# Latent attention's deferred layer-norm scale and shift: four 128x1024 passes written for GpSimd instead of VectorE

## What is computed

```python
def layer_norm(x, g, b):
    xf = x.astype(F32)
    mu = jnp.mean(xf, -1, keepdims=True)
    var = jnp.mean(jnp.square(xf - mu), -1, keepdims=True)
    return ((xf - mu) * lax.rsqrt(var + LN_EPS) * g + b).astype(x.dtype)

def modulated_sublayer(x, mod, g, b, fn, res_w):
    shift, scale, gate = mod[:, 0, None, :], mod[:, 1, None, :], mod[:, 2, None, :]
    y = fn(x * (1.0 + scale) + shift)
    return layer_norm(DEEPNORM_ALPHA * x + res_w * (1.0 + gate) * y, g, b)

def mla(h, pos, w_down, q_norm, kv_norm, w_uq, w_ukv, w_out):
    cq, ckv, kr = jnp.split(h @ w_down, [C_Q_RANK, C_Q_RANK + C_KV_RANK], axis=-1)
    q = (rms_norm(cq, q_norm) @ w_uq).reshape(bsz, seq, C_HEADS, C_NOPE + C_ROPE)
    kv = (rms_norm(ckv, kv_norm) @ w_ukv).reshape(bsz, seq, C_HEADS, C_NOPE + C_V)
    ...   # rope on part of q and on kr, softmax attention over 16 heads, two blocks of 128 queries
    return o.swapaxes(0, 1).reshape(bsz, seq, C_HEADS * C_V) @ w_out
```

## Time and profile before

| what | value |
|---|---|
| time, median of 3 runs | 1033.8 us (1032.54 to 1034.34) |
| span of the profiled execution | 1031.5 us |
| PE busy in the span | 999.8 us (97%) |
| DVE busy | 805.0 us (78%) |
| ACT busy | 501.1 us (49%) |
| POOL busy | 47.5 us (5%) |
| latent attention, from its first transposes to the next sublayer's | about 721 to 841 us of the span |

### The profile page before, as it was taken

The page is one execution under the profiler, slowest core; times in us unless marked ns, Lnnn a source line. Parts: engine busy times, 40 slices in busy tenths (PEclk is TensorE's granted clock), DMA queues, the critical chain, the costliest instruction groups (busy, mean ns, idle before and its releaser), DMA issues.

```text
span 1031.5 us, 13182 instructions
## 1 busy us (share of the span) xinstructions
PE 999.8 (97%) x5024; PEld 830.8 (81%) x5024; DVE 805.0 (78%) x1192; ACT 501.1 (49%) x749; POOL 47.5 (5%) x101
## 2 busy tenths in 40 slices
PE   7999999999999999999999999999999999999996
PEld 5678888879978788888887888888878878888885
DVE  5989898678989888888879788877787786666455
ACT  3654344376767534343445343443666654443430
POOL 1000000002311000000000000000000010000000
PEclk9999999999999999999999999999999999999998
DMA  9999998458423699979758987972323449756431
GB/s 353 409 352 410 386 374 321 152 184 287 164 95 125 210 370 350 329 272 341 272 176 332 328 304 277 387 261 93 97 93 123 166 166 312 239 199 245 163 123 41
DMA packets 72545, 254.80 MB, mean 247 GB/s; under 512 B 8801, under 2 KB 10337, under 8 KB 72482
## 3 DMA queue, kind: packets, MB, share of 16 engines
q1 hardware_dynamic: 68946, 242.91, 65.4%
q0 software_dynamic: 3104, 10.39, 3.1%
q10 hardware_dynamic: 432, 0.66, 0.2%
HBM read 252.85 MB, written 1.07 MB: 246 GB/s over the span
## 4 chain that ended last, share of the span: by engine, by line
PE 81%; DVE 7%; ACT 4%; issue 3%; DMA 3%; SPq 0%; POOL 0%; DVEq 0%; ACTq 0%; POOLq 0%
PE bank L1769 25%; PE bank L1773 25%; PE bank L1772 25%; DMA w_raw<-in_w_dram 2%; PE bank L2170 2%; DMA arena<-in_ada_w_dram 1%; DVE w_lo L1156 1%; ACT w_hi L851 1%; PE bank L1995 1%; ACT arena L866 1%; PE bank L1913 1%; PE bank L1880 1%; PE bank L1764 1%; PE bank L2025 0%; DVE arena L1173 0%
## 5 line engine op out<-in xcount | busy, mean ns | idle before, releaser
L1156 DVE TENSOR_TENSOR w_lo<-w_raw,w_hi 128x2048 fp32r<-128x2048 f32 (+3 forms) x161 | 345.0, 2162 | 27.6 <-ACT w_hi L851 27.6
L1769 PE MATMUL bank<-w_hi,hT_hi 128*128 128x512 f32 (+3 forms) x880 | 350.0, 398 | 12.7 <-DVE hT_lo L1201 6.2
L1773 PE MATMUL bank<-w_lo,hT_hi 128*128 128x512 f32 (+3 forms) x880 | 338.8, 385 | 0.0
L1772 PE MATMUL bank<-w_hi,hT_lo 128*128 128x512 f32 (+3 forms) x880 | 338.4, 385 | 0.0
L851 ACT ACTIVATE w_hi<-w_raw 128x2048 fp32r<-128x2048 f32 (+3 forms) x152 | 281.1, 1852 | 36.0 <-DMA w_raw<-in_w_dram 25.8
L1769 PEld LDWEIGHTS bank<-w_hi,hT_hi 128*128 128x128 f32 x880 | 166.0, 189 | 48.4 <-DVE hT_lo L1201 7.4
L1773 PEld LDWEIGHTS bank<-w_lo,hT_hi 128*128 128x128 f32 x880 | 165.8, 188 | 33.2
L1772 PEld LDWEIGHTS bank<-w_hi,hT_lo 128*128 128x128 f32 x880 | 166.4, 189 | 28.8
L936 ACT ACTIVATE arena<-bank 128x256 f32<-128x256 f32 x88 | 33.7, 383 | 290.2 <-PE bank L1773 290.1
L1173 DVE SCALAR_TENSOR_TENSOR arena<-arena,c_row 128x1024 f32<-128x1024 f32 x131 | 155.9, 1219 | 8.4 <-DMA arena<-in_ada_w_dram 8.3
L1769 PE MATMUL bank<-w_hi,fT_hi 128*128 128x512 f32 x352 | 138.1, 392 | 0.9 <-DVE fT_lo L1679 0.9
(11 more groups left out here) (235 smaller groups left out, 858.0 us busy)
## 6 DMA issues: line engine op xcount, KB each, us to landing
w_raw<-in_w_dram SPq DMA_DIRECT2D x306, 512.0 KB, 5.5
arena<-in_ada_w_dram SPq DMA_DIRECT2D x132, 512.0 KB, 7.3
m_o<-in_ada_w_dram SPq DMA_DIRECT2D x10, 512.0 KB, 7.1
gate_row<-gate_scratch POOLq DMA_DIRECT2D x6, 512.0 KB, 4.8
arena<-in_ln_g_dram POOLq DMA_DIRECT2D x6, 512.0 KB, 4.9
arena<-in_ln_b_dram POOLq DMA_DIRECT2D x6, 512.0 KB, 6.9
w_raw<-in_w_dram SPq DMA_DIRECT2D x8, 256.0 KB, 2.8
w_raw<-in_w_dram SPq DMA_DIRECT2D x8, 192.0 KB, 2.8
```

What stands on the lines that cost most here:

```text
L1156: op = nc.vector.tensor_tensor(w_lo[:, j0 % RING, c], raw_of(j0)[:, c], w_hi[:, j0 % RING, c].bitcast(F32), ALU.subtract)
L1769: mm = nc.tensor.matmul(dst, a_hi, b_hi, start=start, stop=False)
L1772: nc.tensor.matmul(dst, a_lo, b_hi, start=False, stop=False)
L1773: return nc.tensor.matmul(dst, a_hi, b_lo, start=False, stop=stop)
```

## The change

The stage `scale` is taken out of VectorE's list and put into GpSimd's. The four operations, their shapes and their operands are the same.

```diff
                             nc.gpsimd.tensor_tensor(rms[:, 2 * t:2 * t + 2], ssq[:, 2 * t:2 * t + 2],
                                                     neg_half[:, 0:1].broadcast_to([P, 2]), ALU.pow).then_inc(rms_ready, 1)
+                        elif stage == "scale":
+                            t, part = m
+                            pool.wait_ge(n_tr, 4 * s + 2 * t + 2)
+                            pool.wait_ge(ln_rows_in, 32 * s)
+                            step.wait()
+                            op = nc.gpsimd.tensor_tensor(x[:, t, :], x[:, t, :], ln_rows[:, part, :], (ALU.mult, ALU.add)[part])
+                            if part == 0:
+                                step(op)
+                            else:
+                                op.then_inc(x_ready, 1)
                 ln_tail(s)
...
                     elif stage in ("split", "lo"):
                         split_lo(base[s] + m[0], m[1:])
-                    elif stage == "scale":
-                        t, part = m
-                        if part == 0:
-                            dve.wait_ge(ln_rows_in, 32 * s)
-                            step(nc.vector.tensor_tensor(x[:, t, :], x[:, t, :], ln_rows[:, 0, :], ALU.mult))
-                            scaled = step.n
-                        else:
-                            dve.wait_ge(dve_step, scaled)
-                            nc.vector.tensor_tensor(x[:, t, :], x[:, t, :], ln_rows[:, 1, :], ALU.add).then_inc(x_ready, 1)
                     elif stage == "end":
```

## The result

The changed kernel takes **1039.96 us** (median of 5 runs, 1037.95 to 1040.89) against 1033.93 (5 runs beside it): 1.0056 times as long, 95% interval 1.0046 to 1.0067. It is slower by 6.0 us, where 2.8 were forecast; the time lies 1.2 us above the end of the range.

A forecast was written before the change was run, and what follows sets the result against it. TensorE, busy for 97% of the span, was taken as the bound. A slip of +4.0 us from two held rotations less a gain of 1.2 gave +2.8, so 1036.6 us, range 1032.4 to 1038.8.

The forecast's parts named there:

- the gain: Before the transposes at 762.82 us, TensorE's 1.17 us gap closes once VectorE's passes go: 1.2 us gained, bounds 0 and 2.2.
- The cause and its places: GpSimd's reads hold VectorE's two-SBUF-input operations; TensorE idles about 2 us before the product at 743.93 and the transposes at 748.65.
- The first pass: From 742.71 us it holds VectorE's L1608 in the first rotation by 2.0 us; TensorE's product at 743.93 slips by 2.0.
- The passes' length: Each 128x1024 two-input pass on GpSimd takes 2.2 us, between 1.2 and 2.44.
- The second rotation: It begins at 748.3 us; the third pass holds its L1608 by 2.0; the transposes at 748.65 slip 4.0 in all.
- The held remainder: Weight remainder L1156, 745.29 us before, waits for the second pass until 747.4 and ends at 748.3; costed at nothing by itself.
- the rival of three holds: Third pass admitted before the second rotation, fourth before its L1608: 6.0 - 1.2 = +4.8 us, 1038.6; chance 0.13.
- The scans of the earlier trace: VectorE's L1422 took 0.68 to 0.90 us beside GpSimd's L787 at 0.55 to 1.42; read as GpSimd losing more.
- The rival of hardly any loss: VectorE's operations win nearly each time and its slack takes in the rest; only the gain stays: -1.2 us, 1032.6; chance 0.20.
- one hold only: First pass enters after L1608; only the second rotation's L1608 is held, by 2.0 us: +0.8 us, 1034.6; chance 0.22.

The follow-up runs named there:

- e2: The changed kernel with GpSimd's four passes left out and four fills of 128x2048 that only write SBUF in their place: 1032.53 us.
- e3: The kernel before, VectorE keeping its passes, with four operations of the same shape added on GpSimd, whose results nobody needs: 1041.49 us.
- e5: The changed kernel with each GpSimd pass made to wait for the maximum of a later attention step (9, 10, 11 and 14): 1032.41 us.
- e7: The changed kernel with each GpSimd pass cut into two operations of 512 columns, eight in all: 1036.79 us.
- e4: The changed kernel with 12 and 20 extra TensorE products in front of the two places where it waits for VectorE: 1038.79 us.
- e11: The changed kernel as it is, run once more without extra products: 1039.12 us.
- the half change: The change for the first tile alone: GpSimd does the first two passes, VectorE keeps the last two where they were: 1035.58 us.

## Why the prediction was wrong

*What bounds the kernel, and the gain: right.* The gap of 1.17 us closed and nothing else did; 1.2 was forecast, the kernel without passes gives 1.4 and the marks 1.34.

*The cause and its places: right.* VectorE's rotations are held in the two stretches named, and TensorE waits at the two instructions named. The holds come from GpSimd's reads (e2 and e3).

*The first pass: right in size.* Forecast 2.0, measured 2.17 on TensorE. GpSimd got in one operation earlier, between the two L1606 (the second starts at 743.97 and takes 2.39 us) and not in the pause before L1609: here VectorE operations that follow closely were no protection.

*The passes' length: mis-sized a little.* 2.2 us was taken; a pass beside which VectorE read PSUM or stood idle took 2.35 to 2.40 (e5), near the upper end of 2.44. The fixed part of the operation is small: two of 512 columns take 2.52 us (e7).

*The second rotation: the step that failed.* The forecast let one pass, the third, hold this rotation, by 2.0 us, and put the fourth, which was to meet the next weight remainder, at nothing. Instead the third pass got in ahead of the rotation's first operation (L1604, +1.63) and the fourth between its next two (L1606, +2.20). So the rotation lost 3.83 us, and TensorE's transposes slipped by 6.4 instead of 4.0. The held remainder (+1.12) is not part of the miss: the forecast had the rotation begin behind it, at 748.3, and the remainder ended at 748.56 when the 1.16 us of the first mark are taken off. Nor are the 0.48 us in which the rotation waited for ScalarE's L1017: with the clock kept up (e4) that wait is gone, L1604 starts at 749.62 and takes 2.48 instead, and the transposes start when they did.

That is the rival of three holds, priced at +4.8; without the clock the marks give 6.44 - 1.34 = 5.1. It was given a chance of 0.13 because its admission seemed to need a narrow moment. Here it needed none: each pass was admitted at the next boundary between VectorE's operations, the third as soon as the held remainder had ended. The Trainium skill's rule (SBUF — State Buffer, Who interferes with whom), that the shared pair of ports is an exclusive lock, was the better guide: by it at its hardest the prediction had all four passes hold VectorE, for 8.8 us; they held it four times, for 7.1.

The scans of the earlier trace rows had made GpSimd look like the one that waits. The two lines shown there are not of one moment: L787's are from 269.6 to 273.1 us, L1422's from 256.9 to 259.0. The scans that ran beside those L787, from 269.5 to 271.4 us, took 0.68 to 0.82 us, so GpSimd did lose more than VectorE there; the reading stands, but it did not carry over. The scans are of about the length of GpSimd's operation beside them, while a pass is several times as long as a rotation operation; that this makes the difference was not tested.

*The clock: a term that was missing.* TensorE's new waits bring its clock down to the lower level twice in the first profile; the fall behind the second wait costs 1.3 to 1.5 us where it comes, the one behind the first wait is hidden by the holds of VectorE's second rotation (e4, e11). Together the slip is 4.9 us without the second fall (e11) and 6.4 with it (first profile); the medians of two sets of runs lie 6.0 and 5.7 above the kernel before. So the holds alone miss the forecast of 2.8 by some 2 us, and the clock adds the rest where it falls.

*The rival of hardly any loss* has fallen; *one hold only* was in effect measured by the half change, 1.9 instead of the 0.8 that it was given; the fall of the clock, 1.60 in its profile, had no term there either.

## What to carry to other kernels

An idle engine is not a free one: before two-input work is moved to GpSimd, look at what VectorE runs in that moment, operation by operation, and count one of its operations with two SBUF inputs as held, for the rest of a GpSimd operation that reads, by each such GpSimd operation. Gate such work to moments in which VectorE reads PSUM or waits, or leave it on VectorE and move it to one of its idle places, which here gave the same 1.3 to 1.6 us. And a new wait on TensorE costs more than its length if its clock falls behind it and no later wait hides that (2.16 us for the wait and 1.60 for the clock in the profile of the half change).

## What the runs showed of the hardware that was not expected

- A GpSimd operation with two SBUF inputs was admitted between two directly following VectorE operations, and a pair of 64-column operations then took 2.5 us instead of 0.35. A fill of 1.8 us beside the same operations cost them nothing.
- An unhindered fp32 operation of 128x1024 with two inputs took 2.35 to 2.40 us on GpSimd, of 128x512 some 1.26, of 128x256 (int32, before the change) 0.61.
- With waits of 2.5 and 2.7 to 3.0 us, TensorE's granted clock fell to about half behind the first one in both profiles of the changed kernel, behind the second in one of the two.
